# Two of the four token-half sums of each FFN on GpSimd, and the first feature tile's taps moved ahead on VectorE

## The reference, cut to what matters

```python
def causal_dwconv(x, prev, w):
    T = x.shape[1]
    xp = jnp.concatenate([prev.astype(x.dtype), x], axis=1)
    y = xp[:, 0:T] * w[0]
    for k in range(1, CONV_WIDTH):
        y = y + xp[:, k:k + T] * w[k]
    return y, xp[:, T:]

def conv_ffn(h, prev, w_in, conv_w, conv_b, w_out):
    a, v = jnp.split(h @ w_in, 2, axis=-1)
    a, buf = causal_dwconv(a, prev, conv_w)
    return (jax.nn.silu(a + conv_b) * v) @ w_out, buf
```

## Time and profile before

| | us |
|---|---|
| median of 3 runs | 2611.71 |
| lowest and highest | 2608.33, 2614.79 |
| the profiled execution | 2607.61 |
| its span, from the first to the last instruction | 2605.8 |
| TensorE busy | 2471.6 (95%) |
| VectorE busy | 1590.7 (61%) |
| ScalarE busy | 931.1 (36%) |
| GpSimd busy | 140.4 (5%) |

### The profile page before, as it was taken

The page is one execution under the profiler, slowest core; times in us unless marked ns, Lnnn a source line. Parts: engine busy times, 40 slices in busy tenths (PEclk is TensorE's granted clock), DMA queues, the critical chain, the costliest instruction groups (busy, mean ns, idle before and its releaser), DMA issues. The chain is left out here.

```text
span 2605.8 us, 44694 instructions
## 1 busy us (share of the span) xinstructions
PE 2471.6 (95%) x19150; PEld 2319.6 (89%) x19150; DVE 1590.7 (61%) x2384; ACT 931.1 (36%) x1553; POOL 140.4 (5%) x214
## 2 busy tenths in 40 slices
PE   7999999899999999999999999789899999989997
PEld 5888999899999989998985777569899999989996
DVE  6422246787777765765354445977787777764553
ACT  4210124533333334543333554034533233334442
POOL 1000000000000010000002000210000000010000
PEclk8999999999999999999999999899899999999998
DMA  9677232222222266553210032882223222255563
GB/s 348 221 256 269 84 111 87 78 90 74 74 74 88 70 213 192 174 170 122 70 33 21 21 142 100 339 290 81 70 74 95 77 74 74 76 195 173 185 185 108
DMA packets 325190, 343.70 MB, mean 132 GB/s; under 512 B 14701, under 2 KB 297106, under 8 KB 312381
## 3 DMA queue, kind: packets, MB, share of 16 engines
q1 hardware_dynamic: 301393, 205.48, 25.7%
q0 software_dynamic: 23600, 135.35, 13.7%
HBM read 289.19 MB, written 51.82 MB: 131 GB/s over the span
## 5 line engine op out<-in xcount | busy, mean ns | idle before, releaser
L1530 DVE TENSOR_TENSOR w_lo<-w_raw,w_hi 128x1024 fp32r<-128x1024 f32 (+1 forms) x198 | 227.2, 1159 | 216.8 <-ACT w_hi L1026 216.0
L1026 ACT ACTIVATE w_hi<-w_raw 128x1024 fp32r<-128x1024 f32 (+1 forms) x198 | 197.3, 1005 | 316.0 <-DMA w_raw<-in_ffn_w_out 151.4
L2412 PE MATMUL ps<-h_hi,w_hi 128*128 128x344 f32 x816 | 267.0, 327 | 7.5 <-DVE h_lo L1649 3.4
L2414 PE MATMUL ps<-h_hi,w_lo 128*128 128x344 f32 x816 | 263.1, 322 | 0.0
L2413 PE MATMUL ps<-h_lo,w_hi 128*128 128x344 f32 x816 | 263.0, 322 | 0.0
L2471 PE MATMUL ps<-h_hi,w_hi 128*128 128x344 f32 x608 | 197.6, 325 | 1.8 <-DVE h_lo L1718 1.5
L2473 PE MATMUL ps<-h_hi,w_lo 128*128 128x344 f32 x608 | 195.1, 321 | 0.0
L2472 PE MATMUL ps<-h_lo,w_hi 128*128 128x344 f32 x608 | 194.9, 321 | 0.0
L1285 ACT ACTIVATE op_hi_Y<-op_raw_Y 128x512 fp32r<-128x512 f32 x80 | 50.6, 632 | 332.7 <-DVE op_raw_Y L1949 170.4
L2412 PEld LDWEIGHTS ps<-h_hi,w_hi 128*128 128x128 f32 x816 | 155.7, 191 | 13.8 <-issue 4.3
L2414 PEld LDWEIGHTS ps<-h_hi,w_lo 128*128 128x128 f32 x816 | 155.6, 191 | 0.0
(11 more groups left out here) (402 smaller groups left out, 6274.4 us busy)
## 6 DMA issues: line engine op xcount, KB each, us to landing
w_raw<-in_ffn_w_out SPq DMA_DIRECT2D x96, 512.0 KB, 4.1
mod_late<-in_mod_w SPq DMA_DIRECT2D x40, 1024.0 KB, 9.7
fr<-in_ffn_w_in SPq DMA_DIRECT2D x80, 512.0 KB, 4.8
act_d<-g_sb POOLq DMA_DIRECT2D x36, 516.0 KB, 5.8
w_raw<-in_ffn_w_out SPq DMA_DIRECT2D x48, 384.0 KB, 3.4
xc<-x_d POOLq DMA_DIRECT2D x12, 1376.0 KB, 7.5
x_d<-xc POOLq DMA_DIRECT2D x9, 1376.0 KB, 5.4
w_raw<-in_sc_w_in SPq DMA_DIRECT2D x24, 512.0 KB, 3.8
```

Source lines behind the costliest of these rows:

```text
L1026: act.activation(w_hi[k.slot][:, 0:k.kt, :], w_raw[k.slot][:, 0:k.kt, :], ACT.Copy).then_inc(hi_ready, 1)
L1530: dve.tensor_tensor(w_lo[k.slot][:, 0:k.kt, :], w_raw[k.slot][:, 0:k.kt, :], w_hi[k.slot][:, 0:k.kt, :].bitcast(F32), ALU.subtract).then_i ...
L2412: pe.matmul(o, w_hi[k.slot][:, t, :], h_hi[:, t, up_cols(c)], start=t == 0, stop=False)
L2414: ins = pe.matmul(o, w_lo[k.slot][:, t, :], h_hi[:, t, up_cols(c)], start=False, stop=t == KD - 1)
```

## The change

In each FFN, Z5 (both instructions) and Y7 leave VectorE's list and go to GpSimd's, into a function `row_sums(l)` between `down_moves` and `store_g`. GpSimd waits for `h_ready` and, ahead of Y7, for the same `w_done` as before. VectorE does the taps of tile 0 first, as soon as `a_e` is up, and then waits for `sr_ready` to be 2 (mod 4), that is for GpSimd's Y7, before it forms Y6. The sizes, the operands and all other orders stay.

```diff
@@ GpSimd
+            def row_sums(l):
+                w1 = 2 * UC - HT
+                pool.wait_ge(h_ready, NU * (2 * l + 2))
+                pool.tensor_tensor(s_raw["Z5"][:, :, 0:w1], r21[:, :, 0:w1], r22a[:], ALU.add)
+                pool.tensor_tensor(s_raw["Z5"][:, :, w1:HT], r21[:, :, w1:HT], r22[:, :, w1:HT], ALU.add).then_inc(sr_ready, 1)
+                pool.wait_ge(w_done, blocks[first[f"f{l}"] + 1].done)
+                pool.tensor_tensor(s_raw["Y7"][:], r11[:], r21[:], ALU.subtract).then_inc(sr_ready, 1)
...
             down_moves(0)
+            row_sums(0)
             store_g("f0", KF, KEPT)
...
             down_moves(2)
+            row_sums(1)
             store_g("f1", KF, KEPT)
@@ VectorE
                 conv_start(NU * (2 * l + 2))
                 lo_to(n0 + 2 * NPL - 1)
-                step(dve.tensor_tensor(s_raw["Z5"][:, :, 0:w1], r21[:, :, 0:w1], r22a[:], ALU.add))
-                dve.tensor_tensor(s_raw["Z5"][:, :, w1:HT], r21[:, :, w1:HT], r22[:, :, w1:HT], ALU.add).then_inc(sr_ready, 1)
-                dve.wait_ge(w_done, blocks[n0 + 1].done)
-                dve.tensor_tensor(s_raw["Y7"][:], r11[:], r21[:], ALU.subtract).then_inc(sr_ready, 1)
-                settle()
+                dve.wait_ge(a_e, AE0[stage] + 1)
+                conv_f(0)
                 dve.wait_ge(sr_ready, 4 * l + 2)
                 dve.tensor_tensor(s_raw["Y6"][:], s_raw["Z5"][:], r11[:], ALU.subtract).then_inc(sr_ready, 1)
-                dve.wait_ge(a_e, AE0[stage] + 1)
-                conv_f(0)
                 dve.wait_ge(sr_ready, 4 * l + 3)
```

## The result

The changed kernel takes 2631.6 us (median of 7 runs, 2626.07 to 2640.7), the kernel before 2614.79 us (7 runs, 2604.25 to 2622.65). The ratio is 1.0073, with a 95% interval of 1.0056 to 1.009: slower by 14.6 to 23.5 us. The profiled execution of the changed kernel took 2626.07 us, its span is 2624.3 us, 18.5 us over the span of before.

A forecast was written before the change was run, and what follows sets the result against it. TensorE, 2471.6 of 2605.8 us, was taken as the bound. Lateness of 13.7 us plus 4.6 us of half clock made 18.3 us, added to the median of 2611.7 for 2630.0 us; range 2617 to 2638.

The forecast's parts named there:

- Where to look, and that nothing could be won: TensorE's waits from 503 to 650 us: 2.9 us, at most 5.8 us over both FFNs, 0.2%, too little to see.
- Y6 as the hinge: Silu stands behind ScalarE's copies of Y6 and Z5, so Y6's time counts; 8.46 us from Y6's start to TensorE's column.
- The 0.7 us that s4_raw was to give back: From Y6 to TensorE's column: 8.46 us instead of 9.18, since s4_raw held the gate before.
- The price of a sum: Z5 and Y7 on GpSimd: 4.3 us a sum, between 3.4 and 5.2; 8.7 us for both, against 4.7 on VectorE.
- Sums and taps one after the other: GpSimd's sums and VectorE's taps exclude each other: 8.7 + 3.5 + 0.3 us of hand-overs before Y6 starts.
- The column: TensorE's v-column of tile 1 starts 7.0 us late in the first FFN, 6.65 in the second, together 13.7.
- The clock: TensorE at half clock after idling 7.45 and 6.65 us: 2.3 us lost in each FFN, between 1.5 and 3.0.
- The later waits of 1.1 and 0.7 us: TensorE's later waits of 0.7 and 1.1 us stay, since their work stands behind VectorE's gate of tile 1.
- The sum: Whole kernel: 13.7 + 4.6 = 18.3 us slower, median 2630.0 us, this case spanning 2625 to 2635; chance 0.66.
- Side by side: Rival: GpSimd's sums and VectorE's taps don't hold each other up; about 10 us slower, 2614 to 2627 us; chance 0.20.
- Not slower: Rival: GpSimd ends Y7 by the time the taps end, sums of 2.7 us or less; 2611.7 us; chance 0.05.
- More than counted: Rival: half clock lasts longer or hand-overs exceed 0.1 us; another 3 us per FFN, 2636 us and above; chance 0.09.

The follow-up runs named there:

- e8: Kernel before, all sums on VectorE, reordered: Z5, taps, gate, Y7, Y6, s4_raw, with ScalarE's silu ahead of its copies; 2610.18 us, ratio 0.9992.
- e1: Kernel before with only the order changed: VectorE takes tile 0's taps ahead of Z5 and Y7, which stay on VectorE; 2629.94 us, ratio 1.0054.
- e3: Changed kernel with Y7 back on VectorE ahead of the taps, only Z5 on GpSimd; 2631.27 us, ratio 1.007.
- e2: Changed kernel with the taps back behind Y6 on VectorE, Z5 and Y7 still on GpSimd; 2626.85 us, ratio 1.0048.
- e4: Changed kernel with ScalarE's silu of tile 0 ahead of its copies of Y6 and Z5; 2624.9 us, ratio 1.0038.
- e7: e4 with tile 0's gate also put ahead of s4_raw on VectorE, straight behind Y6; 2624.87 us, ratio 1.0034.
- e6: Changed kernel with GpSimd forming Y7 twice into the same place, one after the other; 2638.85 us, ratio 1.0103.
- e5: Changed kernel with 44 needless matmuls on TensorE ahead of its wait for tile 0's gate, in both FFNs; 2625.77 us, ratio 1.0051.

## Why the prediction was right

**Where to look, and that nothing could be won.** The waits of TensorE made 2.9 us in the first FFN, of which 0.45 at the gate. The prediction took the second FFN to be the same; the gate's wait was missing there, which makes the upper bound of what could be won smaller still. e8 takes the gate's wait away altogether and measures no change. Right.

**Y6 as the hinge.** From Y6's start to TensorE's column the prediction had 8.46 us; measured are 523.55 - 515.11 = 8.44, and 8.44 again in the second FFN, in e1 and in e3. The 0.7 us that s4_raw was to give back are there too: where the taps stand behind Y6 (e2), it is 9.18. e1 shows the hinge from the other side, taps ready early with nothing won. Y6 is the hinge only in this order: e4 takes the two copies out from between Y6 and the gate, e7 s4_raw too, and in e8 the gate doesn't wait for Y6 at all.

**The price of a sum.** 4.3 us was the middle of bounds of 3.4 and 5.2 that came from a memset; measured are 4.70, and 4.73 for Z5 (507.21 - 502.48, start to start). The two sums took 9.4 us and not 8.7. The term was too small by 0.7 us. The Trainium skill's figure in "GPSIMD Engine Reference", section 3.1 (4497 ns for 2048 elements), was nearer: scaled to 2064 elements, an estimate, it gives 4.5, and the trace has 4.70.

**Sums and taps one after the other.** The prediction had 12.5 us from GpSimd's start to Y6 (8.7 + 3.5 + 0.3); measured are 515.11 - 502.48 = 12.63. That this is so near is luck in part: the sums took 0.7 more, and what stood behind them took 515.11 - 511.91 = 3.2 us instead of 3.8, because the copy of ten elements had ended with Z5 and the tensor_scalar needed only 0.55 us once Y7 was through. The exclusion itself is shown several times: the copy and the tensor_scalar in the changed kernel, the second instruction of Z5 and the copy in e3, and the copy of eight elements in e6 each ended their own length, or less, behind the end of the other engine's instruction (the copy in e3 at 512.09, 0.03 behind GpSimd's); and in e2, where the same taps and sums are kept apart, they have their own lengths. The prediction left open which instructions would stand still; it was the copy and the tensor_scalar, and the two taps with two inputs came after all sums. Of the two places that it read before, only that of 1426.03 had a length to compare with. GpSimd's addition of 16 elements (1.27 us) runs once in each kernel and meets VectorE in every profile, so that GpSimd stands for VectorE too was inferred there; e3 shows it (5.21 us for 3.13). The rule of the Trainium skill in "SBUF — State Buffer", section on who interferes with whom, covers the copy and the tensor_scalar too: it says that they can run in modes that use both ports of VectorE, and contend with GpSimd when they do. The trace agrees for the tensor_scalar as far as it shows: alone it does 1024 elements in 0.75 us, 0.73 ns each, a sum takes 1.11 ns each, and beside GpSimd it stood. The copies stood too, but are too short to tell a mode from.

**The column.** 7.0 and 6.65 us late were predicted, 7.11 and 6.72 measured. TensorE's idle time was put at 7.45 and 6.65, and is 7.50 in both: in the second FFN a_sb, and with it the a-column, came 0.9 us earlier than in the kernel before.

**The clock.** 2.3 us in each FFN were predicted, as the middle of 1.5 and 3.0; 2.28 and 2.73 were measured, and e5 shows them to be the clock's alone (0.00 and 0.01 with the idle stretch filled). The middle of two stretches of another stage, twice apart, is a guess that came out well; that it lies so near in the first FFN is luck. The later waits of 1.1 and 0.7 us stayed, as said.

**The sum.** 13.7 + 4.6 = 18.3 predicted, 13.8 + 5.0 = 18.8 by "late" and "clock", 17.7 by the stages. The medians differ by 16.8 us; 2630.0 was forecast and 2631.6 measured, with a median of before that came out 3.1 us higher in this comparison (2614.79) than in the runs the prediction started from (2611.71).

**The rivals.** Side by side (2614 to 2627) falls with the stretched instructions. Not slower falls with them and with the 4.70 us. More than counted had a mechanism, half clock that lasts longer after a longer stretch: in e6 the stretches are 12.0 and 11.1 us and the costs 2.12 and 2.85, in the changed kernel, at 7.5 us, 2.28 and 2.73. Its other mechanism, longer hand-overs, isn't there either: GpSimd starts 0.08 us behind the last h_lo, and the sum of sums, taps and hand-overs came to 12.63 us for 12.5. It falls as well.

## What to carry to other kernels

Before work is moved to an idle engine, find the instruction that the present order leaves as the last to be ready ahead of the bottleneck's next work (here Y6, because the silu stands behind its copy) and time that, with the engines that exclude each other counted one after the other: the relieved engine here waited as long as GpSimd worked, which was twice as long as the work had taken before. Then look at how much wait of the bottleneck there is to win (0.45 us here, in one FFN of two) beside what a delay costs, which is more than its length: in this kernel 4 to 12 us of idle cost another 2 to 3 us of half clock.

## What was not expected of the hardware

- **Who goes first when both wait.** When Z5 ended in the changed kernel, VectorE's tensor_scalar (recorded from 507.19) and GpSimd's Y7 (from 507.21) both came up, and GpSimd's went first: 5.27 us for the one, 4.70 for the other. In e3 VectorE's Y7 had been waiting since 506.67 when GpSimd's instruction ended at 506.88, and VectorE's went first; in e6 the tensor_scalar, waiting since 507.31, got in between GpSimd's two sums. These three fit an order in which the one that stands waiting goes before the one that comes later. That is only argued: no run here varies the order of arrival by itself.
- **How small an instruction can stand.** Copies of 10 and of 8 elements (0.17 and 0.16 us by themselves) took 2.76, 3.12 and 4.68 us beside a sum of GpSimd. In none of these does the profile count the time as idle.
- **The clock after idle stretches.** The twelve idle stretches of 4.2 to 12.0 us in the ledger are each followed by 4.1 to 6.1 us in which the matmuls come 0.29 us apart and not 0.16; that cost 1.9 to 2.9 us, with no trend in the length of the stretch. After 2.59 us idle (e7) the fall came only after the restart, and cost 1.6; after 1.63 us it cost 0.1.
